# One 8 KB transfer per expert weight matrix in place of two of 4 KB, issued when its whole buffer is free

## What is computed

```python
scores = sigmoid(xf @ w_router)                 # (1024, 64), the 8 chosen are kept
def body(acc, blk):                             # a block: up to 128 rows of one expert
    rows, rw, e = blk
    xb = x_pad[rows]
    h = silu(xb @ w_gate[e]) * (xb @ w_up[e])   # (128, 1024) @ (1024, 256), twice
    yb = (h @ w_down[e]) * rw[:, None]          # (128, 256) @ (256, 1024)
    return acc.at[rows].add(yb), None
shared = (silu(xf @ ws_gate) * (xf @ ws_up)) @ ws_down
```

## Time and profile before

| what | us |
|---|---|
| median of 3 runs | 2026.01 |
| the runs | 2014.58, 2026.01, 2034.15 |
| profiled execution, its span | 2024.6 |
| TensorE busy, of the span | 1834.1 |
| VectorE, ScalarE, GpSimd busy | 1169.8, 900.8, 471.2 |
| DMA: bytes moved, mean rate | 384.85 MB, 190 GB/s |

### The profile page before, as it was taken

One profiled execution on the slowest core, in us unless ns is written; L12 is line 12 of the kernel. 1 busy time (PEld: TensorE's weight loads), 2 busy tenths in 40 slices (PEclk: granted clock), 3 DMA queues, 4 the chain that ended last, 5 costly groups with the idle time before them and its releaser, 6 DMA issues.

```text
span 2024.6 us, 30936 instructions
## 1 busy us (share of the span) xinstructions
PE 1834.1 (91%) x8994; PEld 1469.5 (73%) x8995; DVE 1169.8 (58%) x1612; ACT 900.8 (44%) x1193; POOL 471.2 (23%) x517
## 2 busy tenths in 40 slices
PE   7998999999999979989899999999999999999910
PEld 5896777777777658767787877888778777777700
DVE  3102545644654678773656677655665677668737
ACT  3201322332231433333566677655665667668612
POOL 0020000000000022443233344333333334434303
PEclk9997999999999989889999999999999999999965
DMA  5221011101100244345989999999999999999882
GB/s 174 62 61 32 6 27 31 31 6 26 31 6 5 74 165 150 133 162 173 325 240 301 307 351 342 306 281 294 299 300 282 299 305 330 349 307 353 296 288 92
DMA packets 146255, 384.85 MB, mean 190 GB/s; under 512 B 33824, under 2 KB 58400, under 8 KB 146208
## 3 DMA queue, kind: packets, MB, share of 16 engines
q1 hardware_dynamic: 113840, 270.67, 37.2%
q0 software_dynamic: 32368, 113.56, 21.3%
HBM read 306.39 MB, written 77.79 MB: 190 GB/s over the span
## 4 chain that ended last, share of the span: by engine, by line
PE 66%; DMA 13%; DVE 7%; issue 6%; ACT 3%; POOLq 2%; ACTq 2%; POOL 1%; SPq 0%; another core or an unknown queue 0%; DVEq 0%
DMA x_rows<-rows_scratch,gidx 7%; PE out_ps L844 6%; PE bank L935 5%; PE bank L938 5%; PE bank L941 5%; PE bank L69 5%; PE bank L71 4%; PE bank L70 4%; PE k_ps L961 3%; PE k_ps L962 3%; PE k_ps L966 3%; DMA raw_gu<-in_moe_w_up_dram 3%; PE q_ps L71 2%; PE q_ps L69 2%; PE q_ps L925 2%
## 5 line engine op out<-in xcount | busy, mean ns | idle before, releaser
L935 PE MATMUL bank<-gu_hi,xb_hi 128*128 128x512 f32 x824 | 335.9, 408 | 4.1 <-DVE gu_lo L1546 2.7
L1546 DVE TENSOR_TENSOR gu_lo<-raw_gu,gu_hi 128x1024 fp32r<-128x1024 f32 x260 | 306.8, 1220 | 37.5 <-ACT gu_hi L1166 34.7
L938 PE MATMUL bank<-gu_lo,xb_hi 128*128 128x512 f32 x824 | 327.1, 397 | 0.0
L1166 ACT CAST gu_hi<-raw_gu 128x1024 fp32r<-128x1024 f32 x260 | 253.5, 1049 | 13.6 <-DMA raw_gu<-in_moe_w_gate_dram 8.8
L941 PE MATMUL bank<-gu_hi,xb_lo 128*128 128x512 f32 x824 | 209.0, 395 | 0.0
L935 PEld LDWEIGHTS bank<-gu_hi,xb_hi 128*128 128x128 f32 x824 | 156.8, 190 | 38.8 <-issue 2.1
L588 POOL DMA_INDIRECT sums_scratch<-ys,sidx x95 | 164.1, 1727 | 80.6 <-POOL sidx L585 70.7
L941 PEld LDWEIGHTS bank<-gu_hi,xb_lo 128*128 128x128 f32 x824 | 154.4, 187 | 37.8
L938 PEld LDWEIGHTS bank<-gu_lo,xb_hi 128*128 128x128 f32 x824 | 156.2, 190 | 33.2
L961 PE MATMUL k_ps<-dn_hi,ht_hi 128*128 128x512 f32 x412 | 172.0, 418 | 1.2 <-ACT ht_hi L1195 1.2
L1101 ACT ACTIVATE probs<-bank 128x512 f32<-128x512 f32 (+2 forms) x150 | 73.9, 505 | 209.8 <-PE bank L830 186.4
(11 more groups left out here) (268 smaller groups left out, 3824.0 us busy)
## 6 DMA issues: line engine op xcount, KB each, us to landing
raw_gu<-in_moe_w_gate_dram SPq DMA_DIRECT2D x128, 512.0 KB
raw_gu<-in_moe_w_up_dram SPq DMA_DIRECT2D x128, 512.0 KB
raw_dn<-in_moe_w_down_dram SPq DMA_DIRECT2D x128, 512.0 KB
wqk<-in_fox_w_in_dram SPq DMA_DIRECT2D x16, 512.0 KB, 5.2
fin<-sums_scratch SPq DMA_DIRECT2D x16, 512.0 KB, 10.4
sums_scratch<-zeros POOLq DMA_DIRECT2D x11, 512.0 KB, 8.0
xs<-in_x_dram SPq DMA_DIRECT2D x8, 512.0 KB, 7.0
wv<-in_fox_w_in_dram SPq DMA_DIRECT2D x4, 1024.0 KB, 7.1
```

What stands on the lines that cost most here:

```text
L935: i = pe.matmul(o3, xb_hi[s][:, c], g_hi[:, :, c], start=c == 0, stop=False, skip_group_check=True)
L938: pe.matmul(o3, xb_hi[s][:, c], g_lo[:, :, c], start=False, stop=False, skip_group_check=True)
L1166: a.copy(hi, raw).then_inc(S[done], 1)
L1546: dve.tensor_tensor(lo, raw, hi, ALU.subtract).then_inc(S[lo_ok], 1)
```

## The change

Each gate, up or down matrix is loaded by one transfer. The loads wait for the last piece of the buffer part that they overwrite: piece 1 for gate, piece 3 for up, the second for down. The semaphores get 16 per matrix in place of 32, and the waits on them follow. What ScalarE and VectorE do, and in what order, is the same.

```diff
             def load_gate_up(par, gate, up, left):
 
-                for k in range(G_PIECES):
-                    left(k)
-                    chunks = slice(k % 2 * (DC // 2), (k % 2 + 1) * (DC // 2))
-                    w = (gate, up)[k // 2].rearrange("(p c) n -> p c n", c=DC)[:, chunks]
-                    sp.dma_start(raw_gu[par][:, k // 2, chunks], w).then_inc(g_raw[par][k // 2], 16)
+                for j, w in enumerate((gate, up)):
+                    left(2 * j + 1)
+                    sp.dma_start(raw_gu[par][:, j], w.rearrange("(p c) n -> p c n", c=DC)).then_inc(g_raw[par][j], 16)
 
             def load_down(par, down, left):
-                for k in range(D_PIECES):
-                    left(k)
-                    sp.dma_start(raw_dn[par][:, k], down.rearrange("(p c) n -> p c n", c=FC)[:, k]).then_inc(d_raw[par], 16)
+                left(D_PIECES - 1)
+                sp.dma_start(raw_dn[par][:], down.rearrange("(p c) n -> p c n", c=FC)).then_inc(d_raw[par], 16)
...
-                    act.wait_ge(g_raw[par][k // 2], 16 * (e + 2 - par) + 32)
+                    act.wait_ge(g_raw[par][k // 2], 8 * (e + 2 - par) + 16)
...
-                act.wait_ge(d_raw[1 - par], 8 * D_PIECES * (e + par) + 16 * D_PIECES)
+                act.wait_ge(d_raw[1 - par], 8 * (e + par) + 16)
```

More of the change, by code:

```diff
@@ L1181, in _ @@
             for k in range(G_PIECES):
-                act.wait_ge(g_raw[0][k // 2], 32)
+                act.wait_ge(g_raw[0][k // 2], 16)
                 w_high(g_piece, "g_hi_ok", 0, k)
@@ L1236, in _ @@
                     x1t_hi_of(TT - 1)
-                    act.wait_ge(d_raw[0], 16 * D_PIECES)
+                    act.wait_ge(d_raw[0], 16)
                     for k in range(D_PIECES):
```

## The result

The changed kernel takes 2040.83 us in the median of 20 runs (2032.37 to 2048.83), the kernel before 2029.67 us in 20 (2014.58 to 2042.20). The ratio is 1.0061, with a 95% interval of 1.0040 to 1.0082: 0.6% slower, some 12 us, where +35 us was forecast. The profiled execution after has a span of 2036.3 us, 11.7 more than before. Two executions of the experiments further down, one of e3_8k_plain at 5927 us and one of e5_down8k at 6347 us, were in a slow state and are left out of their ratios.

A forecast was written before the change was run, and what follows sets the result against it. The expert stage was taken as bound by TensorE, with DMA transfers near their limit. Waits for rows 43 us, less 4 packet gain and 4 given back, make +35 on 2026: 2060 us; range 2012 to 2095, the forecast's own 2040 to 2080.

The forecast's parts named there:

- the long waits: TensorE's waits behind two scatters and two gathers end to end: 3.4 us more than counted, three such, 10 us.
- the short waits: Second gather before a two-block expert starts 0.2 us later and takes 1.2 more; thirteen waits, 18 us.
- One packet of 8 KB: Weight loads: one 8 KB packet takes 0.31 us against 0.32 for two of 4 KB; 4 us gained.
- The turn grows: DMA engines: each gather or scatter-add beside queued weights takes 1.2 us more; gross 43 us lost.
- The waits at q_ps: Transposes of an expert's first block, in one-block runs with one scatter ahead: 4 x 2.4 = 10 us.
- The near misses: Gathers just in time now, in the second of two one-block experts, about five: some 1 us each, 5 us.
- Late issue costs nothing: Loads wait for the whole buffer, costed at nothing; 5 us in the last one-block run if the queue were empty.
- Given back: TensorE's row waits give transfers time, and last-stretch idle time can't be paid twice: 4 us taken off.
- the one in which the turn doesn't grow: Rival, chance 0.30: DMA engines cut 8 KB pieces or share by bytes; 2022 to 2030 us, within 1%.
- its second case: Counted within that rival's 0.30: the turn grows but the waits move by less than half.
- The filled software queue: Rival, chance 0.12: gather and scatter delays carry between experts; most of 33 one-block experts wait 1 to 2 us; 2100 us.
- The case for "faster": Rival, chance 0.10: packet gain reaches the path everywhere and the later up load frees engines for late gathers; 1996 us.

The follow-up runs named there:

- e3_8k_plain: The changed kernel with a scatter that only writes instead of adding; ratio 0.9987 to the kernel before.
- e5_down8k: The kernel before with only the down matrix in one 8 KB-packet transfer, issued late; gate and up as before; ratio 1.0008.
- e1: The kernel before, still two 4 KB transfers per matrix, but both issued only when the whole buffer is free; ratio 0.9979.
- e6: Against the kernel before: four 2 KB transfers per matrix, all issued once the whole buffer is free; ratio 0.9969.
- e10: The changed kernel, with VectorE splitting the fourth gate/up piece before the product with silu, so the up load starts earlier; ratio 1.0049 to the kernel before.
- e7: The kernel before, with weight loads from the second expert on moving only 16 of 128 partitions, in 4 KB packets; ratio 0.9808.
- e8: The changed kernel, with weight loads after the first expert's moving only 16 of 128 partitions, in 8 KB packets; ratio 0.9820 to the kernel before.

## Why the prediction was wrong

The direction held, and so did the mechanism at the long waits; the size did not, +11 us in the medians against +35, and what happens at the short waits was wrong. By the prediction's own steps:

1. *One packet of 8 KB.* Right: it exists and takes 0.31 us. The gain in the transfers' own time is real (the DMA share of the hardware queue fell from 37.2% to 35.5%).

2. *The turn grows.* Right: 0.65 us with a scatter against 0.64 predicted, and counts stay equal. Its four terms, 43 us together, came to 14.1 (13.8 with the first wait of the stage, which is 0.3 shorter):
 - The short waits, 13 at 1.4 us, 18 us in all. **This is the step that failed:** "Where the hardware queue is empty nothing changes; at the places that count it isn't." The eleven short waits fell from 16.0 to 12.7 us. At ten of them it is 8.2 us in the mean from the issue of the gather to the transposes, where it was 8.5 before and the prediction's own sign was 9 or more (at the eleventh, near 1199, it is 10.7 for 7.4, and TensorE comes 3.5 us later itself). The account that fits the packets: the queue was full in the kernel before because it was served slowly; with 8 KB per turn the weights are through sooner, and the queue then runs low. Beside the first of the two gathers weights take 19% of the engines' time in the mean (38% before), beside the second, the one waited for, 46% (54% before), and that one moves in 2.97 us (3.06 before), not in 3.9. None of these eleven is among the 30 gathers that meet hardly any weights, so the queue at these places is emptier, not empty. 30 gathers became 27 with the early up load, but 12 with 4 KB and the late issue: the packet does it. A longer turn for some gathers was bought with an emptier queue for others. What was constant was the work, not the queue. (The term has a small slip too: 3.86 less 3.53 us is 0.3, not 0.2.)
 - The long waits: 3 at 3.4 us over the 1.4, 10 us. Two grew by 2.95 and 2.6 us, not 4.8: at the first of them the gathers begin 1.0 us later after their issue (6.46 us for 5.48), and the two, which took 2.9 and 3.0 us to move, take 3.8 and 3.9. The third candidate, near 1769, grew by 0.3 us.
 - The waits at q_ps: 10 us predicted. The four waits grew from 5.1 to 10.0 us, half of it.
 - The near misses: 5 us predicted. Six new waits at q_ps have 5.3 us and two new ones at out_ps 1.7. Right in size.

3. *Late issue costs nothing.* Right in the time, by e1 and e6, and by e10 for the up load; in e1 the short waits are 3.9 us longer all the same.

4. *SyncE.* Right: it waits 671 us of the stage for gate and up buffers.

5. *Given back,* 4 us. Right in size: TensorE's waits at bank (5.3 us at L935 and L949, all in the last run of one-block experts) went to 0.2. Waits at q_ps, 2.2 us, took their place there, and four experts became 3.4 us faster. The chain there goes now through gathers, 11 us from issue to landing where the up loads took 18.90 us:

```profile
1884.94 11.03 DMA x_rows<-rows_scratch,gidx
```

A term that the sum didn't have has the other sign: TensorE is at 1.2 GHz for 34 us of the expert stage in place of 10 (below), and the same matmuls are busy 7.5 us longer. So the 16.5 us of the stage are 14.1 more for rows, 5.1 less at bank, and 7.5 of busy time. That the forecast isn't further off is luck: what it added up came to 9 us, and the clock, which it left out, brought nearly as much again.

Of the rivals, the one in which the turn doesn't grow fell by the packets. But its second case, that the turn grows and the waits move by less than half, is what happened: 14.1 of 43 us, and a result within 1% of the kernel before, at the other side of it than its 2022 to 2030 us. The filled software queue did not come about; that the emptier hardware queue prevents it is argued, not shown. The late weights vanished altogether. The case for "faster" is nearer than I had it, but at the other end: the smaller packet, not the larger, made the kernel faster. The Trainium skill, in "DMA: Bandwidth & Descriptors", section "Rules for kernel authors", asks for 1 MiB or more per transfer for the best bandwidth. Here the kernel was 0.4 to 0.5% faster with transfers of 256 KB than with 512 KB, and 0.6% slower with 1 MB, since the engines' turns, not the rate of one transfer, decided.

What stays open: the split into waits and clock comes from one execution of each kernel, and no run held the clock fixed on purpose. Nor is it shown why the clock fell after one wait and not after another of the same length. And the size of a packet and of its transfer change together in every run: no run has large transfers of small packets, and only e7 and e8 bear on the transfer alone.

## What to carry to other kernels

Where bulk loads and latency-bound gathers share the DMA engines, the size of the bulk packet sets the gathers' share in this kernel: give the loads that have slack the smaller packet, down to where their own overhead starts to be waited for (here 2 KB, with 1 KB too small). Price a changed turn only together with what it does to the length of both queues; a queue that is full before need not be full after. And when an added wait falls where another one was, count the difference.

## What the runs showed of the hardware that was not expected

**A wait of about 2 us can be followed by a fall of TensorE's clock.** In the changed kernel the granted clock falls to 1.2 GHz eight times in the expert stage after its start, for 34 us together, each time within or soon after a wait for rows (of 1.84 to 6.75 us); in the kernel before three times, 10 us together, after waits of 3.80, 4.01 and 2.34 us. At 1309 us it follows a wait of 1.86 us: from the transposes to the next turn of h TensorE then takes 6.3 us (1309.19 to 1315.47), and 4.7 us at the same place before (1306.50 to 1311.19), 1.6 us on top of the wait itself. Not every such wait does it: in e1 one of 3.50 us left the clock alone, in the kernel before those of 1.84 and 2.07 us.

**Packets of several sizes.** In the expert stage the middle packet of weights took 46 ns for 1 KB, 84 for 2 KB, 159 for 4 KB and 309 for 8 KB, which is some 9 ns per packet and 37.5 ns per KB. A scatter that adds takes 327 ns for 4 KB, one that only writes 159.
